# One of the two products that turn the scanned states back moves from VectorE to GpSimd

## The reference

```python
dt = jnp.exp(log_dt.astype(f32))[:, None]
mag = jnp.exp(lam_re * dt)
ar = mag * jnp.cos(lam_im * dt)
ai = mag * jnp.sin(lam_im * dt)
...
xr = jnp.einsum('bsgh,gph->bsgp', u, bbr)
xi = jnp.einsum('bsgh,gph->bsgp', u, bbi)
...
def combine(e1, e2):
    a1r, a1i, b1r, b1i = e1
    a2r, a2i, b2r, b2i = e2
    return (a1r * a2r - a1i * a2i, a1r * a2i + a1i * a2r,
            a2r * b1r - a2i * b1i + b2r, a2r * b1i + a2i * b1r + b2i)

_, _, sr, si = lax.associative_scan(combine, (a_r, a_i, xr, xi), axis=1)
y = (jnp.einsum('bsgp,ghp->bsgh', sr, c_re.astype(f32))
     - jnp.einsum('bsgp,ghp->bsgh', si, c_im.astype(f32))
     + d.astype(f32) * u)
```

## Time and profile before

| | |
|---|---|
| three timed runs | 4036.17, 4036.47, 4031.58 us; median 4036.17 |
| the profiled execution | 4032.52 us, span 4030.7 us |
| busy, share of the span | PE 98%, PEld 83%, DVE 81%, ACT 55%, POOL 27% |
| chain that ended last | PE 90%, DVE 6%, ACT 2%, DMA 1%, issue 1% |
| granted PE clock, mean | 0.998 of full |

### The profile page before, as it was taken

The page is one execution under the profiler, slowest core; times in us unless marked ns, Lnnn a source line. Parts: engine busy times, 40 slices in busy tenths (PEclk is TensorE's granted clock), DMA queues, the critical chain, the costliest instruction groups (busy, mean ns, idle before and its releaser), DMA issues.

```text
span 4030.7 us, 67791 instructions
## 1 busy us (share of the span) xinstructions
PE 3966.3 (98%) x21108; PEld 3332.3 (83%) x21108; DVE 3283.2 (81%) x5720; ACT 2210.8 (55%) x3915; POOL 1106.1 (27%) x1021
## 2 busy tenths in 40 slices
PE   8999999999999999999999999999999999999998
PEld 8978899888888877777779899988888887777776
DVE  6467677985999877999879987688689997777776
ACT  5446544555666655555564465455556665555554
POOL 4100010000122266666620002000012225666662
PEclk9999999999999999999999999999999999999999
DMA  6534655676666688898875544666666668888885
GB/s 225 176 115 143 199 177 189 212 219 206 205 199 198 200 300 287 283 333 310 307 239 179 176 159 153 194 202 213 219 191 199 198 202 280 291 288 305 286 289 185
DMA packets 319525, 899.44 MB, mean 223 GB/s; under 512 B 38256, under 2 KB 105584, under 8 KB 316016
## 3 DMA queue, kind: packets, MB, share of 16 engines
q1 hardware_dynamic: 285728, 812.75, 62.0%
q0 software_dynamic: 28672, 67.27, 5.2%
q10 hardware_dynamic: 4944, 17.06, 1.2%
HBM read 846.61 MB, written 50.33 MB: 223 GB/s over the span
## 4 chain that ended last, share of the span: by engine, by line
PE 90%; DVE 6%; ACT 2%; DMA 1%; issue 1%; DVEq 0%; ACTq 0%; SPq 0%
PE psum L459 12%; PE psum L461 11%; PE psum L460 11%; PE psum L515 9%; PE psum L517 9%; PE psum L516 9%; PE psum L1838 5%; PE psum L1839 5%; PE psum L1840 5%; DVE sb_w_lo L2443 3%; PE psum L2030 2%; PE psum L2032 2%; PE psum L2031 2%; PE psum L450 2%; PE psum L525 1%; DMA sb_raw<-in_v 1%
## 5 line engine op out<-in xcount | busy, mean ns | idle before, releaser
L2119 ACT CAST sb_w_hi<-sb_raw 128x512 fp32r<-128x512 f32 x2736 | 1691.9, 622 | 1536.6 <-PE psum L517 503.8
L2443 DVE TENSOR_TENSOR sb_w_lo<-sb_raw,sb_w_hi 128x512 fp32r<-128x512 f32 x2736 | 1916.4, 733 | 668.5 <-ACT sb_w_hi L2119 660.7
L459 PE MATMUL psum<-sb_w_hi,sb_act_hl 128*128 128x512 f32 x2048 | 800.2, 391 | 5.2 <-DVE sb_w_lo L2443 4.9
L461 PE MATMUL psum<-sb_w_lo,sb_act_hl 128*128 128x512 f32 x2048 | 799.2, 390 | 0.0
L460 PE MATMUL psum<-sb_w_hi,sb_act_hl 128*128 128x512 f32 x2048 | 798.2, 390 | 0.0
L515 PE MATMUL psum<-sb_w_hi,sb_act_hl 128*128 128x512 f32 x1792 | 707.3, 395 | 10.0 <-DVE sb_w_lo L2443 8.4
L517 PE MATMUL psum<-sb_w_hi,sb_act_hl 128*128 128x512 f32 x1792 | 698.0, 390 | 0.0
L516 PE MATMUL psum<-sb_w_lo,sb_act_hl 128*128 128x512 f32 x1792 | 697.6, 389 | 0.0
L2376 POOL TENSOR_TENSOR sb_work<-sb_scratch,sb_work 128x512 f32 x128 | 173.3, 1354 | 1400.0 <-ACT sb_scratch L589 1400.0
L459 PEld LDWEIGHTS psum<-sb_w_hi,sb_act_hl 128*128 128x128 f32 x2048 | 384.8, 188 | 86.8 <-DVE sb_w_lo L2443 6.2
L1838 PE MATMUL psum<-sb_act_hl,sb_w_hi 128*128 128x256 f32 x1488 | 429.4, 289 | 26.5 <-DVE sb_w_lo L2443 13.8
(11 more groups left out here) (396 smaller groups left out, 4828.9 us busy)
## 6 DMA issues: line engine op xcount, KB each, us to landing
sb_raw<-in_u SPq DMA_DIRECT2D x512, 512.0 KB, 3.7
sb_raw<-in_v SPq DMA_DIRECT2D x512, 512.0 KB, 5.0
sb_raw<-in_w_z SPq DMA_DIRECT2D x82, 512.0 KB, 3.8
sb_raw<-in_w_gates SPq DMA_DIRECT2D x64, 512.0 KB, 3.6
acts_mid<-sb_up_acts SPq DMA_DIRECT2D x124, 256.0 KB, 5.0
sb_raw<-in_w_proj SPq DMA_DIRECT2D x56, 512.0 KB, 4.2
sb_raw<-in_w_q SPq DMA_DIRECT2D x48, 512.0 KB, 3.9
sb_raw<-in_w_branch SPq DMA_DIRECT2D x32, 512.0 KB, 4.1
```

Of the source, the lines that this page charges most:

```text
L459: pe.matmul(ps, h, w_hi[:, c, :], start=k == 0, stop=False)
L461: return pe.matmul(ps, h, w_lo[:, c, :], start=False, stop=k == 15)
L2119: act.copy(w_hi[:, c, :], raw[:, 2 * par + c // 2, (c % 2) * 512:(c % 2) * 512 + 512]).then_inc(hi_ready, 1)
L2443: dve.tensor_tensor(w_lo[:, c, :], raw[:, 2 * par + c // 2, (c % 2) * 512:(c % 2) * 512 + 512], w_hi[:, c, :].bitcast(F32), ALU.subtract). ...
```

## The change

`y_cos` is made by POOL, `y_sin` by DVE as before. POOL waits for the same semaphores as DVE did: `s_ready` of set j (the scans are done), `sum_ready` (an earlier use of the rows of y is over) and `ys_done` (PE has used the previous y). Both engines now add one to `ys_in`, so everyone who waited for n sets now waits for 2n: PE before `outputs`, DVE before it overwrites `crossed` in the next `rotate`, ACT before its last taps and high parts, SP before it reloads a table.

```diff
@@ pe_s5, outputs(j)
-                pe.wait_ge(ys_in, j + 1)
+                pe.wait_ge(ys_in, 2 * j + 2)
@@ last_tap, act_s5 (two places)
-                act.wait_ge(ys_in, 8)
+                act.wait_ge(ys_in, 16)
@@ dve_s5, rotate(j)
-                    dve.wait_ge(ys_in, j)
+                    dve.wait_ge(ys_in, 2 * j)
@@ dve_s5, turn_back(j)
-                dve.tensor_tensor(y_cos, crossed, cs, ALU.mult)
                 dve.tensor_tensor(y_sin, crossed, sn, ALU.mult).then_inc(ys_in, 1)
@@ table_back(j)
-                    sp.wait_ge(ys_in, j - 1)
+                    sp.wait_ge(ys_in, 2 * j - 2)
@@ gpsimd
+            def turn_back(j):
+                pool.wait_ge(s_ready, j + 1)
+                pool.wait_ge(sum_ready, 6)
+                if j:
+                    pool.wait_ge(ys_done, j)
+                cs = cos_t[j % 2].unsqueeze(2).broadcast_to([P, 4, 2, T])
+                pool.tensor_tensor(y_cos, crossed, cs, ALU.mult).then_inc(ys_in, 1)
+
             for blk in range(2):
+                for j in range(8 * blk):
+                    turn_back(j)
                 for k in range(16):
```

## The result

The changed kernel takes 4052.40 us (median of six runs, 4050.25 to 4054.61); the kernel before, six runs beside it, 4033.78 (4031.58 to 4036.47). The ratio is 1.0045, 95% interval 1.0032 to 1.0058: 18.6 us slower, for eight VectorE instructions fewer. The prediction said 4053 and +17. The profiled execution has a span of 4050.4 us.

A forecast was written before the change was run, and what follows sets the result against it. PE, busy 98% of the span, bounds the kernel. Group terms in z2, 9.6 + 3.2 + 1.8 + 2.3, give about +17 us: 4049.5 from the profiled 4032.52, 4053 with the timed median's 3.6 more; range 4038 to 4068.

The forecast's parts named there:

- the relief: In z2, eight products (17.6 us) leave VectorE; PE's waits for low parts shrink, 6.7 us gained if nothing else happened.
- rival (a): GpSimd's long product in z2 is served in gaps, without a real hold, and VectorE is relieved: -8 us, 4028; chance 0.07.
- The product: GpSimd's 128x2048 product in z2 takes 4.7 us, by the slope of its shorter rows; 3.0 and 5.9 kept as bounds.
- rival (c): GpSimd is much slower on this strided view in z2, product 7.8 us: +36 us, 4072; chance 0.08.
- The hold: In z2 a VectorE instruction reading two SBUF tiles stands while GpSimd reads: 4.7 us lost to save 2.2.
- Rival (b): GpSimd's reading in z2 yields in pieces, each low part some 1.2 us late: +8 us, 4044; chance 0.13.
- plain set: z2 groups j = 1, 2, 3, and 6 the same: the second low part is held, PE waits 2.9 us, +3.2 each.
- T: End of VectorE's second set of scans in each z2 group; period 27.5 us before, predicted 30.7 after.
- slow passage: 15 PE matmuls at half clock (213 ns apart) behind a long wait in z2, priced at 1.4 us each.
- Set 0: First z2 group: VectorE's own product goes first, the hold falls on later low parts, PE's slack takes a part: +1.8 us.
- Sets 5 and 7: z2 groups: in 5, L1115 and L1117 lie beside the hold; in 7 it precedes the convolution; 0 us each.
- Set 4: z2 group j = 4: gate work lying beside the hold takes about one off, +2.3 us.

The follow-up runs named there:

- experiment 1: Cosine product left out on both engines, otherwise as the change; against the kernel before: 4022.62 against 4034.11 us, 0.9969.
- experiments 4 and 5: Kernel before plus, on GpSimd, an extra 768-column product (4041.16 against 4034.11 us, 1.0018) or a memset of the same columns (4034.35 against 4033.33, 1.0002).
- experiment 5: Kernel before, VectorE making both products, plus a GpSimd memset of 768 columns that only writes: 4034.35 against 4033.33 us, 1.0002.
- experiment 2: The change with GpSimd's product cut into four pieces of 512 columns; against the kernel before: 4044.97 against 4034.11 us, 1.0029.
- experiment 10: Against the kernel before, GpSimd makes half the cosine product (1024 columns) in sets 0 to 6, beside VectorE's PSUM work: 4029.30 against 4033.92 us, 0.9990.

## Why the prediction was right, point by point

**The bound, the relief.** PE's waits for low parts are the only thing that VectorE's relief can touch: right. Its size was low: 8 at most in rival (a), 10.4 measured in experiment 1. The 6.7 of waits was right; 2.2 of slow matmuls went, not 1.4, and 1.5 is left that I can't place.

**The product.** 4.7 predicted, 4.53 to 4.64 where it ran without VectorE ahead of it. The slope of GpSimd's own shorter rows was the right choice; 3.0 and 5.9 were both far off, and rival (c) fell with them. The Trainium skill (GPSIMD Engine Reference, Elementwise — side-by-side cycle accounting) has 4497 ns for an add of this size; the shortest here is 4534.

**The hold.** Right: one instruction of VectorE stands until GpSimd ends, in every set. In set 7 it is one of the convolution's (six L1585 in 6.82, 2.95 when free). Rival (b), a hold in pieces, fell: in sets 0, 1 and 6 one low part takes 5.0 to 5.1, not four 1.8 each. Rival (a) fell with it; experiments 4 and 5 isolate it as reading.

**Where the hold lands.** I had it between the first and the second low part in each plain set. That holds for set 1 alone. At set 2 a small instruction stood there first, at set 3 three low parts passed before GpSimd got in, and at set 6 GpSimd came 0.08 us ahead of the first low part, so that the first was held (timelines after):

```profile
2202.68 4.54 POOL L2368 TENSOR_TENSOR sb_work<-sb_work 128x2048 f32<-128x2048 f32 x1 [25.96 <-DVE sb_work L1562]
2202.70 4.55 DVE L1097 SCALAR_TENSOR_TENSOR sb_work<-sb_work 128x8 f32<-128x8 f32 x1
...
2234.65 1.89 DVE L2452 TENSOR_TENSOR sb_w_lo<-sb_raw,sb_w_hi 128x512 fp32r<-128x512 f32 x3
2234.76 6.25 POOL L2368 TENSOR_TENSOR sb_work<-sb_work 128x2048 f32<-128x2048 f32 x1 [27.53 <-DVE sb_work L1562]
...
2237.07 4.50 DVE L2452 TENSOR_TENSOR sb_w_lo<-sb_raw,sb_w_hi 128x512 fp32r<-128x512 f32 x1 [0.53 <-ACT sb_w_hi L2118]
...
2329.10 4.54 POOL L2368 TENSOR_TENSOR sb_work<-sb_work 128x2048 f32<-128x2048 f32 x1 [26.02 <-DVE sb_work L1562]
2329.18 5.02 DVE L2452 TENSOR_TENSOR sb_w_lo<-sb_raw,sb_w_hi 128x512 fp32r<-128x512 f32 x1
```

The periods of T grew by 3.7, 4.6 and 1.7 in sets 1 to 3, 9.9 in sum where I had 9.6. The sum was right by luck, and its terms were not: which instruction is held, and so which quarter PE gets late, differs from set to set. In set 3 PE waited only 0.92 and 0.45 and the clock stayed up; its +1.7 is near the +1.8 that the prediction had for a period without a slow passage.

**Set 0, 5 and 7.** Set 0: +1.8 predicted and measured; GpSimd's span there is 6.72, because VectorE's own product went first and held it. Sets 5 and 7: 0 each; -1.8 and +0.3 measured. L1115 and L1117, from PSUM, were not held, as the sum took it; the first low part behind them lost the rest (set 5, after, against the earlier trace rows):

```profile
2298.32 2.13 DVE L1115 SCALAR_TENSOR_TENSOR sb_near<-psum,sb_work 128x128 f32<-128x128 f32 x8
2300.37 0.68 DVE L1117 TENSOR_REDUCE sb_work<-psum 128x4 f32<-128x512 f32 x1
2301.08 4.35 DVE L2452 TENSOR_TENSOR sb_w_lo<-sb_raw,sb_w_hi 128x512 fp32r<-128x512 f32 x4
```

**Set 4, the mis-sized term.** I had +2.3, "a group of gate work that now lies beside the hold"; it measured +5.8. The gate work was not beside the hold but behind it:

```profile
2263.88 4.54 DVE L1108 TENSOR_TENSOR sb_work<-sb_work 128x8 f32<-128x8 f32 x1
2268.45 1.66 DVE L1110 TENSOR_SCALAR sb_turn<-sb_consts,sb_work 128x128 f32<-128x128 f32 x8
2270.02 2.49 DVE L2452 TENSOR_TENSOR sb_w_lo<-sb_raw,sb_w_hi 128x512 fp32r<-128x512 f32 x4
```

An instruction of 128x8, 0.17 us when free, stands ahead of L1110, was held for 4.5, and the gate work and all four low parts queued behind it: PE's longest wait, 5.43. Set 6 also cost more than planned, 4.9 for 3.2. The two misses, +3.5 and +1.7, are offset only by set 5 (-1.8); with small ones the profile has 20.9 against the 16.9 predicted. The timed medians give 18.6. That the absolute time came out only 0.6 from the 4053 is partly luck: the median before, 4036.17 in the three runs that the prediction started from, is 4033.78 over six.

**The clock.** A slow passage behind a wait of 2.9 us was priced at 1.4 in each of five groups; 60 more slow matmuls are 5.6 us against 5 x 1.4 - 1.4 = 5.6. The sum fits, in part by luck: set 3 had no slow passage, and those behind the waits of 5.43 and 2.75 (set 7) are longer, some 22 and 27 matmuls for the 15. The link to the length of one wait does not fit: in experiment 5 the same matmul has the same wait of 2.44 as in the earlier trace rows, and the clock stays at full (timeline, window):

```profile
2294.85 0.36 PE L1838 MATMUL psum<-sb_act_hl,sb_w_hi 128*128 128x256 f32 x1 [2.44 <-DVE sb_w_lo L2453]
...
2295.00:2298.00 3.00, 3.00 (x26) 1.00 0.81 265
```

What decides it there stays open.

## What to carry to other kernels

Before work goes to an idle GpSimd, look at what VectorE executes in that time: while GpSimd reads SBUF, an instruction with two SBUF inputs stands until GpSimd ends, whatever its own size, and so does everything queued behind it. Put GpSimd's reads beside VectorE instructions that take an input from PSUM, no longer than those, and give it only the share that fits. A saving on the nearly critical engine (17.6 us of instructions, 10.4 of time) must be set against the longest single delay, not only against the sum.

## What the runs showed of the hardware

- A VectorE instruction of 128x8 took 4.54 and 4.55 us beside GpSimd's product of 128x2048; with GpSimd's pieces of 512 columns L1108 took 1.29, and with 768 columns L1097 took 1.85: the length is GpSimd's.
- A `TENSOR_SCALAR` from SBUF to SBUF (L1110, 0.2 us each) was held too: three of eight took 1.25 to 1.30 in experiment 2. It has one SBUF tile as input and a column of scalars. One of them took 0.57 beside a GpSimd memset, which only writes (experiment 5), where a low part and L1097 kept their lengths. So it is held otherwise than they are; the runs don't show by what.
- In these traces the turning products, with one input in PSUM, were never stretched: 2.28 us beside GpSimd's 2.41 (experiment 10). Nor were L1115 and L1117 (2.13 and 0.68 beside GpSimd's 4.60 in set 5).
- When VectorE streams without a gap, GpSimd sometimes gets in after the first low part, sometimes only where VectorE pauses, as at 2236.5 in set 3: its record is then longer (6.25), and the hold comes all the same. That its reading began only there is worked out from this length.
- GpSimd's fp32 product took 1.24 us for 512 columns (four in 4.95), 1.85 for 768, 2.41 for 1024 and 4.53 for 2048.
